# A two-layer encoder trunk on one core: square sums by TensorE, and the stages before them put in another order

## What is computed

```
def _modulate(x, c, g, w, b):
    m = (c @ w + b)[:, None, :]
    shift, scale, gate = jnp.split(m, 3, axis=-1)
    return _rmsnorm(x, g) * (1.0 + scale) + shift, 1.0 + gate

h, gate = _modulate(x, c, norm_g[i, 0], ada_w[i, 0], ada_b[i, 0])
x = x + gate * mixer(h)          # layer 0: _ab_mixer, layer 1: attention
h, gate = _modulate(x, c, norm_g[i, 1], ada_w[i, 1], ada_b[i, 1])
x = x + gate * (jnp.square(jax.nn.relu(h @ w1)) @ w2)
```

## Time and profile before

| | |
|---|---|
| device time, median of 3 runs | 1287.99 us (1287.62 to 1291.09) |
| the profiled execution's own time | 1290.38 us |
| its span, first to last instruction | 1288.6 us |
| PE busy in the span | 1241.1 us (96%) |
| DVE, ACT, GpSimd busy | 761.0, 448.7, 94.8 us |
| mean granted TensorE clock | 0.984 of full speed |

### The profile page before, as it was taken

One profiled execution on the slowest core, in us unless ns is written; L12 is line 12 of the kernel. 1 busy time (PEld: TensorE's weight loads), 2 busy tenths in 40 slices (PEclk: granted clock), 3 DMA queues, 4 the chain that ended last, 5 costly groups with the idle time before them and its releaser, 6 DMA issues.

```text
span 1288.6 us, 16165 instructions
## 1 busy us (share of the span) xinstructions
PE 1241.1 (96%) x6192; PEld 1004.8 (78%) x6192; DVE 761.0 (59%) x1041; ACT 448.7 (35%) x611; POOL 94.8 (7%) x128
## 2 busy tenths in 40 slices
PE   6999599999999999999999998999999999999999
PEld 3788588788888888888779885567788888888887
DVE  7898777754654645655468957864643443443432
ACT  5442412421422312323443247862432231331321
POOL 0010012000000000051000001114100000000022
PEclk9999799999999999999999998999999999999999
DMA  9558755544445444431223220003143223223311
GB/s 322 187 116 261 244 192 197 172 160 154 146 168 171 171 163 131 171 112 58 83 70 122 82 89 1 1 1 98 33 131 98 76 98 92 92 98 98 98 65 65
DMA packets 132686, 157.40 MB, mean 122 GB/s; under 512 B 19784, under 2 KB 113152, under 8 KB 132608
## 3 DMA queue, kind: packets, MB, share of 16 engines
q1 hardware_dynamic: 125328, 153.82, 36.4%
q10 hardware_dynamic: 7312, 2.96, 1.1%
HBM read 151.39 MB, written 4.19 MB: 121 GB/s over the span
## 4 chain that ended last, share of the span: by engine, by line
PE 84%; DVE 9%; DMA 3%; ACT 2%; issue 1%; SPq 1%; ACTq 0%; POOL 0%; DVEq 0%
PE psum L1646 83%; PE psum L1650 2%; DVE ada_acc_b L1111 1%; DVE work L1294 1%; DMA ada_first<-in_ada_w 1%; DVE w_lo L1283 1%; DVE h_lo L1304 1%; DVE ada_acc L1111 1%; DMA raw_bn<-in_ssm_b_im 1%; DMA y_scratch<-y_run 1%; ACT pT L1034 1%; SPq L534 0%; DVE s_t L1082 0%; DVE rstd L1111 0%; DVE s_im L1082 0%
## 5 line engine op out<-in xcount | busy, mean ns | idle before, releaser
L1646 PE MATMUL psum<-h_hi,w_hi 128*128 128x512 f32 (+1 forms) x872 | 343.1, 393 | 3.4 <-DVE w_lo L1283 3.3
L1646 PE MATMUL psum<-h_lo,w_hi 128*128 128x512 f32 (+1 forms) x872 | 340.5, 390 | 0.0
L1646 PE MATMUL psum<-h_hi,w_lo 128*128 128x512 f32 (+1 forms) x872 | 340.4, 390 | 0.0
L751 ACT ACTIVATE w_hi<-w_raw 128x2048 fp32r<-128x2048 f32 x92 | 174.3, 1895 | 285.6 <-PE psum L1646 285.0
L1283 DVE TENSOR_TENSOR w_lo<-w_raw,w_hi 128x2048 fp32r<-128x2048 f32 x92 | 213.4, 2320 | 100.2 <-ACT w_hi L751 99.7
L1646 PE MATMUL psum<-a_hi,w_hi 128*128 128x512 f32 x512 | 202.4, 395 | 0.0
L1646 PE MATMUL psum<-a_hi,w_lo 128*128 128x512 f32 x512 | 202.2, 395 | 0.0
L1646 PE MATMUL psum<-a_lo,w_hi 128*128 128x512 f32 x512 | 202.1, 395 | 0.0
L1646 PEld LDWEIGHTS psum<-h_hi,w_hi 128*128 128x128 f32 (+1 forms) x872 | 164.0, 188 | 42.6 <-issue 7.2
L1646 PEld LDWEIGHTS psum<-h_hi,w_lo 128*128 128x128 f32 (+1 forms) x872 | 163.9, 188 | 35.0
L1646 PEld LDWEIGHTS psum<-h_lo,w_hi 128*128 128x128 f32 (+1 forms) x872 | 163.9, 188 | 33.8
(11 more groups left out here) (300 smaller groups left out, 1331.4 us busy)
## 6 DMA issues: line engine op xcount, KB each, us to landing
w_raw<-in_mlp_w SPq DMA_DIRECT2D x64, 1024.0 KB, 5.3
ada_l_ring<-in_ada_w SPq DMA_DIRECT2D x64, 384.0 KB, 6.1
w_raw<-in_cd_w_in SPq DMA_DIRECT2D x14, 1024.0 KB, 5.2
ada_more<-in_ada_w SPq DMA_DIRECT2D x20, 384.0 KB, 4.0
ada_first<-in_ada_w SPq DMA_DIRECT2D x5, 1024.0 KB, 15.4
ada_ring<-in_ada_w SPq DMA_DIRECT2D x12, 384.0 KB, 5.0
w_raw<-in_ab_w_in SPq DMA_DIRECT2D x4, 1024.0 KB, 7.4
w_raw<-in_ab_w_out SPq DMA_DIRECT2D x4, 1024.0 KB, 7.1
```

Source lines behind the costliest of these rows:

```text
L751: act.activation(w_hi[n % 2][:, :, 0:w], raw[n % 2][:, :, 0:w], ACT.Copy).then_inc(hi_ready, 1)
L1646: return nc.tensor.matmul(o, lhsT, rhs, start=start, stop=stop, **kw)
```

## The change

1. Squares: ACT writes the squares of each tile to a work buffer, and PE sums it over the partitions with four matmuls of one column, accumulating in one bank, two tiles late; GpSimd adds nothing there.
2. `kr`: four matrices at a time go to four groups of 32 partitions of one bank, a matmul in each group in turn; ACT copies two groups, DVE the other two, inside `chain(0)`. One semaphore value for all.
3. Ten small matmuls (`WARM`) on PE ahead of the wait for `toep`.
4. `v` is made group by group of channels, copied and used group by group.
5. The band matrices are built in DVE's setup (the first) and after `first_scales` (three), in other places of memory, with fewer instructions.
6. Order of DVE's list: `ada_steps` counts between the stages, 8, 8, 2 and 7 before, become 8, 4, 4 and 3; then 5+2, 3+3, 3+3 and 2 in the output slots instead of 4+3, 4+4, 4+4 and 0.
7. `ada_sums` waits for an earlier count of `mods_part`; units 4, 5 and 6 are summed in output slots 1, 2 and 3.
8. Unit 7 goes into the first quarter of the MLP, which is written out ahead of the loop: its rows are loaded in SP's list between the slots, its 8 steps done in DVE's slots 1, 2 and 3 (2, 3 and 3), its sum made at the end of slot 3.
9. Order of SP's list: row loads and the weights `AB_OUT+1` come after the transfers of `y`.

```diff
+WARM = 10
+    ada_acc_c = place("ada_acc_c", [P, ADA_Q], F32, offset=sumsq_at)
+    LATE_FROM = 40
+    LATE_STEPS = {1: range(0, 2), 2: range(2, 5), 3: range(5, 8)}
+    late_done = [43, 44, 47, 48, 49, 52, 53, 54]
+    def kr_part(q):
+        return bank[0][2 * C * q:2 * C * (q + 1), :]
...
-        load(AB_OUT + 1, slots[AB_OUT + 1])
-        more_ada(3)
         for half in range(2):
             sp.wait_ge(y_copied, 2 * half + 2)
...
-        more_ada(6)
+        more_ada(3)
+        load(AB_OUT + 1, slots[AB_OUT + 1])
+        more_ada(5)
         load(AB_OUT + 2, slots[AB_OUT + 2])
         more_ada(8)
         load(AB_OUT + 3, slots[AB_OUT + 3])
-        more_ada(15)
+        more_ada(8)
...
+        def late_row(j):
+            a, c0, w = ADA_UNITS[7]
+            if j < ADA_RING:
+                sp.wait_ge(ada_used, LATE_FROM - ADA_HOMES + j + 1)
+            else:
+                sp.wait_ge(ada_used, late_done[j - ADA_RING])
+            sp.dma_start(ada_home(LATE_FROM + j), ada_w[0, a, j * P:(j + 1) * P, c0:c0 + w])\
+              .then_inc(ada_in[j % ADA_RING], 16)
...
+                if first:
+                    for j in {0: range(0, 3), 2: range(3, 5), 3: range(5, 8)}.get(i, ()):
+                        late_row(j)
+        quarter(0, 0, first=True)
+        with sp.Fori(1, QUARTERS) as q:
...
-        for k in range(1, SQ):
-            pool.wait_ge(square_in, k)
-            pool.wait_ge(sumsq_ready, k)
-            pool.tensor_tensor(sumsq[:, :], sumsq[:, :], work[1 + 2 * (k % 2)][:, 0:L], ALU.add)\
-                .then_inc(sumsq_ready, 1)
...
-        for b in range(NB):
-            act.wait_ge(v_ps, NB)
-            act.activation(v_tok[:, b, :], bank[4 + b], ACT.Copy).then_inc(v_copied, 1)
+        for g in range(4):
+            act.wait_ge(v_ps, g + 1)
+            act.activation(v_tok[:, :, g * P:(g + 1) * P], bank[4 + g].rearrange("p (b d) -> p b d", d=P), ACT.Copy)\
+               .then_inc(v_copied, 1)
...
+            if half == 0:
+                dve.wait_ge(mats_ps, 9)
+                for q in range(2, 4):
+                    dve.tensor_copy(kr[:, q::4, :], kr_part(q).rearrange("p (t n) -> p t n", n=P))\
+                       .then_inc(kr_ready, 1)
...
+                if first:
+                    for j in LATE_STEPS.get(i, ()):
+                        dve.wait_ge(ada_in[j % ADA_RING], 16 * (3 + j // ADA_RING + 1))
...
-            pe.wait_ge(mods_part, unit if q is not None else unit - (unit > 3))
+            pe.wait_ge(mods_part, part if part is not None else unit if q is not None else max(2, unit - 1))
...
+        def square_sums(k):
+            pe.wait_ge(square_in, k + 1)
+            for b in range(NB):
+                last_ = mm(bank[5][:, b:b + 1], work[1 + 2 * (k % 2)][:, b * P:(b + 1) * P], ones[:, 0:1],
+                           k == 0 and b == 0, False, skip_group_check=True)
+            last_.then_inc(sumsq_ready, 1)
...
+        for t4 in range(GT // 4):
+            for b_, g_ in ((bd[0], g_re), (bd[1], g_ni)):
+                for q in range(4):
+                    t = 4 * t4 + q
+                    mm(kr_part(q)[:, t4 * P:(t4 + 1) * P], b_[:, t, :],
...
+        idle_products(WARM, bank[1])
         pe.wait_ge(toep_in, 16 * 2 * RUN)
...
                 for r in range(2):
                     tile(n, first_tile[n] + r, r)
+                    square_sums(2 * i + r - 2)
                     if r == 0:
-                        ada_sums(8 * (5 + i), 4 + i)
+                        ada_sums(8 * (4 + i), 3 + i)
...
+                if first and i == 3:
+                    ada_sums(ADA_EARLY + late_done[7], 7)
```

More of the change, by code:

```diff
@@ L863, in _ @@
         prep(GLU)
[L864 to L869, removed]
+        act.wait_ge(mats_ps, 9)
+        for q in range(2):
+            act.activation(kr[:, q::4, :], kr_part(q).rearrange("p (t n) -> p t n", n=P), ACT.Copy)\
+               .then_inc(kr_ready, 1)
+        act.wait_ge(kr_ready, 4)
         act.wait_ge(toep_zero, 1)
@@ L949, in quarter @@
                            .then_inc(square_done, 1)
-        with act.Fori(0, QUARTERS) as q:
+        quarter(0, 0)
+        with act.Fori(1, QUARTERS) as q:
             quarter(0, q)
@@ L1290, in _ @@
         first_scales()
+        for g in range(1, 4):
+            make_band(g)
+        dve.sem_inc(bands, 1)
         def scaled(a, k):
@@ L1398, in _ @@
         ada_steps(8)
[L1399 to L1402, removed]
         prep(AB_OUT)
[L1404 to L1409, removed]
+        ada_steps(4)
+        for ct in range(4):
+            gelu_low(ct)
+        ada_steps(4)
         for g in range(4):
@@ L1436, in _, with quarter @@
             prep(n + 1)
-            ada_steps((4, 4, 4, 0)[i])
+            ada_steps((5, 3, 3, 2)[i])
             for r in range(2):
                 residual(first_tile[n] + r, 2 * i + r, 0)
-                if r == 0:
-                    ada_collect(4 + i)
-                    if i == 2:
+                if r == 0 and i:
+                    ada_collect(3 + i)
+                    if i == 3:
                         ada_scale(1, 7)
-                    if i == 3:
-                        ada_gate(1, 8)
                 if r == 0 and i < 3:
-                    ada_steps((3, 4, 4)[i])
+                    ada_steps((2, 3, 3)[i])
         token_rstd(1)
         modulate(1)
-        def quarter(layer, q, last=False):
+        def quarter(layer, q, last=False, first=False):
             n0, t0 = MLP[layer], first_tile[MLP[layer]]
@@ L1465, in quarter @@
                         else:
-                            dve.wait_ge(ada_used, 2 * ADA_STEPS - ADA_EARLY + e + 16 * q)
+                            late = sum(len(v_) for i_, v_ in LATE_STEPS.items() if i_ <= i) if first else 8
+                            dve.wait_ge(ada_used, LATE_FROM + late + e + 16 * q)
                             ins = dve.scalar_tensor_tensor(out=ada_acc[:, :], in0=src,
@@ L1489, in quarter @@
                                       pa[:, bass.ds(q * 6 + 32 + (2 + s) * 24, 6)], A).then_inc(mods_part, 1)
-        with dve.Fori(0, QUARTERS) as q:
+        quarter(0, 0, first=True)
+        with dve.Fori(1, QUARTERS) as q:
             quarter(0, q)
@@ L1946, in a, with quarter @@
             return a_hi[:, k, :], a_lo[:, k, :]
-        def quarter(layer, q):
+        def quarter(layer, q, first=False):
             n0, t0 = MLP[layer], first_tile[MLP[layer]]
@@ L1960, in quarter @@
                         tile(n0 + i, t + r, r, q, moving)
+                if first and i == 3:
+                    ada_sums(ADA_EARLY + late_done[7], 7)
                 if layer == 0 and i % 4 == 3:
-                    ada_sums(2 * ADA_STEPS + 8 * (i // 4 + 1) + 16 * q, 8 + i // 4 + 2 * q, q)
-        with pe.Fori(0, QUARTERS) as q:
+                    ada_sums(2 * ADA_STEPS + 8 * (i // 4 + 1) + 16 * q, 8 + i // 4 + 2 * q, q,
+                             7 if first and i == 3 else None)
+        quarter(0, 0, first=True)
+        with pe.Fori(1, QUARTERS) as q:
             quarter(0, q)
```

111 lines of the change are left out of this document (58 added, 53 removed).

## The result

| | before | after |
|---|---|---|
| device time, median of 20 runs each | 1290.10 us (1286.67 to 1299.89) | 1280.08 us (1275.51 to 1294.78) |
| the profiled execution's own time, span | 1290.38, 1288.6 us | 1277.51, 1275.8 us |
| mean granted TensorE clock in it | 0.984 | 0.988 |

The ratio after to before is 0.9911, with an interval of 0.9884 to 0.9939: faster by 7.9 to 15 us, with 11.5 in the middle (the two medians lie 10.0 us apart). The time forecast was 1271.0 us with a range of 1263 to 1278; the median lies 9 us above the forecast and 2 us outside the range. Two of the 9 us are in the kernel before, whose median was 1287.99 us in the three runs shown and 1290.1 in twenty.

The account below looks back on a forecast made before the run. PE bounds the kernel, busy 1241 of 1289 us, with an 11.5 us wait for `mods` standing out. -22.9 (lead) + 1.3 (sum) + 3.5 (stall) + 1.5 (half clock) = -16.6, say -17: 1288.0 to 1271.0 us, range 1263 to 1278.

Parts of the forecast that it names:

- The path up to `norm(1)`: PE's starts moved one by one: `half_outputs` 102.0, `v` 116.9, GLU ending 136.5, `AB_OUT` 138.4, `norm(1)` sums near 191.
- the wait for `mods`: PE's 11.5 us wait before the output projection, said to be not for the projection's data but for `ada_sums` of unit 3.
- `kr` overlaps in four groups: `kr` on PE falls from 8.35 to 2.8 us; the no-overlap rival, 1276 us, had chance 0.11.
- The lead at `norm(1)`: Gain by the end of the output slots: 24.7 us before them, less 1.8, gives 22.9 us.
- Unit 7 in the first quarter: Rows waiting for DVE delay weights of slots 3 and 4: +3.5 us, +1.5 half clock; full-gain rival, 1266.4 us, chance 0.20.
- the landing time of the two weight loads: First quarter, weights of slots 3 and 4: slot 3's land 5.3 us after issue, at 248.3; slot 4's at 262.
- the half clock behind the stall: First quarter: 1.5 us added because a similar pause of 2.2 us brought the half clock at 129.
- the stall: First quarter: PE waits 2.8 us for unit 7, then 0.7 for the next unit, +3.5 us; bounds 1 to 6.
- the unit sum: Unit 7's sum on PE moves from the output slots to the first quarter, costing 1.3 us as before.
- a clock that stays at half somewhere behind the output slots: Falsifying sign: the prediction is wrong if the clock stays at half somewhere after the output slots.
- WARM "costs nothing": Ten matmuls in the wait for `toep`, 2.2 us, cost nothing unless it lands before; at most 1 us without `kr` overlap.
- GpSimd's additions "hidden, and taking it away gives nothing on PE": Output slots: the last addition ends at 212.2, before PE wants it at 213.67; square sums on PE add 4.2 us.

Follow-up runs that it names:

- experiment 5: Kernel before with only the semaphore value changed: sums of unit 3 and later wait for one unit fewer in `mods_part`; 1282.03 us, ratio 0.992.
- experiment 4: Kernel after with the `kr` matmuls reordered, all eight of one group of 32 partitions before the next group; 1281.63 us, ratio 0.9894.
- experiment 1: Kernel after with unit 7's late rows issued behind the weights of slots 4 and 5 in SP's list; 1268.40 us, ratio 0.9789.
- Experiment 6: Kernel after with no small matmuls ahead of the wait for `toep` (`WARM` 0 instead of 10); 1295.03 us, ratio 1.0005.
- experiment 2: Kernel after with GpSimd adding the squares of the output slots again and no square sums on PE; 1285.11 us, ratio 0.9936.
- experiment 8: Kernel after with late rows behind the weights, plus six GpSimd additions nobody reads, square sums staying on PE; 1269.90 us, ratio 0.9854.
- experiment 9: Kernel after with late rows behind the weights, and GpSimd adding the squares again without square sums on PE; 1272.73 us, ratio 0.9894.
- experiment 11: Kernel before with ten small matmuls added behind its `kr` copies, ahead of its wait for `toep`; 1287.73 us, ratio 0.9982.
- experiment 10: Kernel after with late rows behind the weights and 14 small matmuls instead of 10 ahead of the wait for `toep`; 1268.31 us, ratio 0.9832.
- experiment 7: Kernel after with 24 idle products on PE ahead of unit 7's sum in the first quarter; 1280.95 us, ratio 0.9931.

## Why the prediction was right, and where it was wrong

**The path up to `norm(1)`** was right. The waits were attributed as the prediction read them: the wait for `mods` was a count (experiment 5), `kr` overlaps in four groups (experiment 4), and each start from `half_outputs` to 136.5 us came within half a microsecond (`kr` itself ended 1.1 us sooner than forecast). For `kr` the trace agrees with the Trainium skill ("TensorEngine Tiling (Array Packing)", Theoretical Speedup), up to 4x for stationary tiles of 32 columns: 64 instructions took 1.9 us, 7.4 before. The lead at `norm(1)`, 21.7 us against 22.9, is 1.2 short by the stretch at half clock in the output slots, for which the sum had no term. There is luck in this part too: it held because the ten small matmuls held the clock, which the sum did not count on (see WARM below).

**The step that failed** is "Unit 7 in the first quarter": the mechanism was right and the size was not. The mis-sized terms are the landing time of the two weight loads and the half clock behind the stall. The text had +3.5 for the stall and +1.5 for half clock, with 1.3 for the unit sum 6.3 us in all; the profile has 11.7 (76.62 less 64.95). Moved by the 22.9 us of lead, the prediction's steps can be laid beside the chain of the kernel after:

```profile
220.73 7.79 DMA w_raw<-in_mlp_w
...
236.41 6.63 DMA w_raw<-in_mlp_w
```

The weights of slot 3 were to be issued at 220.1 and were at 220.7. They were to land after 5.3 us, the median of all 64 such loads, and took 7.8 and then 6.6. Two and three rows of 384 KB are issued just ahead of them; with the rows behind (experiment 1) the same two loads took 6.5 and 5.7 us. SP was no slower than forecast: it issued each load 0.4 us after DVE's step, where 0.5 was allowed for the second. The two loads, 2.5 and 1.3 us over their price, are the whole of DVE's lateness: it ends unit 7 at 250.5 instead of 246.7, and the wait is 5.7 us instead of 2.8. The half clock then lasts 10.2 us behind the pause, not some 3: +2.5 us in the two sums (5.1 instead of 2.6) and about +2.4 in twelve products, together 4.9 where the sum had 1.5. This also meets a sign that the prediction had named for being wrong, a clock that stays at half somewhere behind the output slots. Experiment 1 takes the cause away and gets 9.1 of the 11.7 us back in the profile.

**WARM "costs nothing"** was half a reading: what it gives had no term. The prediction saw a clock of 0.50 at 129 us and asked only for the pause next to it. Experiment 6 shows what the matmuls are worth: 12 to 15 us. It bears on the median too. Of the 20 runs of the kernel after, four lie at 1291.6 to 1294.8 us with a mean clock of 0.976 to 0.979, the rest but one at 1275.5 to 1282.1 with 0.987 to 0.993. That the clock fell at the wait for `toep` in those four is argued and not shown, as none of them has a profile. What speaks for it is experiment 6 with the same mean clock, and the profile of experiment 5, whose clock (0.979) falls to 0.50 at 107.9, behind a wait of 0.96 us for `toep`, and is back at about 135 us:

```profile
106.00 5.37 PE L1646 MATMUL psum<-u_run,toep 128*128 128x64 f32 x32 [0.96 <-DMA toep<-kr]
```

The median of the fifteen fastest runs is 1277.9, so these executions move the median by some 2 us. In the kernel before such executions cost less, some 9 us, as far as one can tell because part of it hid in the wait for `mods`: in experiment 5's profile the unit sums come 9.0 us later than in the earlier trace rows, and unit 4's sum 2 us earlier than in the earlier trace rows.

**GpSimd's additions "hidden, and taking it away gives nothing on PE"** was wrong in the new order. The prediction asked when an addition ends, and not what it does to the DVE instruction beside it. Experiments 2, 8 and 9 show the price, 0.6 to 1.04 us on a step, and that it reaches PE only if PE doesn't do the square sums itself. The Trainium skill ("SBUF — State Buffer", Who interferes with whom) has the rule: a DVE instruction with two SBUF inputs contends with a GpSimd instruction that reads SBUF. The trace agrees for the 768-wide step of two inputs (1.01 to 2.05 us). The forecast's time was not hurt by it, since it costed DVE's steps in the slots without such stretching.

**The rest.** Behind the first quarter the lead grows again by 2.8 us (10.1 to 12.8), where the prediction had none. The granted clock has room for all of it: behind 300 us the profiled execution spent 13.7 us at half clock before and 7.2 after, and a stretch at half clock loses at most half its length, so the difference is worth up to 3.3 us. It is no work of the change, as far as one can tell: the kernel before with ten small matmuls (experiment 11) has 3.4 us there, less than the kernel after. By the profiled span the error is 1.2 + 5.4 - 2.8 = 3.8, and with the 0.4 by which -16.6 was rounded to -17 it is the 4.2 us between 1271.6 and 1275.8; the 2.8 are a piece of luck that made it smaller. By the medians it is larger by the baseline's 2 us and the executions at a fallen clock.

**Open:** why a wait of 0.3 to 1 us for `toep` lets the clock fall in some executions and not in others; why it fell without a pause at 172.3 us; whether the rows ahead are all that makes the two loads longer; how much of the first quarter's loss is clock alone.

The best versions are experiments 1 and 10: 1268.4 and 1268.3 us, 2.1% and 1.7% below the kernel before by their ratios.

## What to carry to other kernels

In a queue that also waits for semaphores, what counts for a load is what stands ahead of it: a row that waits for a DVE step makes the weights behind it as late as that step, so put loads on the critical path ahead of transfers that wait, and price them with the traffic they share. A short wait ahead of a stage of small matmuls can cost far more than the wait (3.8 us cost 12 to 15 here); look at the granted clock of the whole stage behind it, and fill the wait before counting its microseconds. Work on an engine that looks idle is free only as long as the engine beside it has slack: read the duration of the neighbour's instruction with and without it.

## What the runs showed of the hardware that was not expected

- Once fallen, the clock stayed at 0.50 through some 30 us of a PE busy without a gap (experiment 6, 104 to 134 us, matmuls of 64 moving columns and 63) and came back during `v`; in the first quarter, with products of 512 columns behind the sums, it was back after 10.2 us.
- The clock also fell with PE busy and no pause ahead: from 172.3 to 175.6 us in the kernel after, 1.6 us lost. The profile of experiment 7 has no such stretch in the output slots.
- An addition of 128 x 512 on GpSimd makes a 768-wide DVE step beside it 1.04 us longer, and this holds for the step with one SBUF tensor too (0.61 to 1.65 us). It was to be read in the trace before, where such a step takes 1.65 us at 195.39 beside the addition at 194.01.
- The order of the matmuls within four groups of partitions decides between 1.9 and 5.9 us for the same 64 instructions (experiment 4).
- A group of eight one-column instructions costs PE 0.81 us before the next work when it stands between products (162.28 to 163.09 us in the kernel after), where 0.84 was worked out from the earlier trace rows.
